# Hybrid encoder on one core: the double weight sum of a seven-product pair ahead of the split, a later DRAM round trip of the hidden tile, and VectorE's order around them

## What is computed

```
x = x + swiglu(rms_norm(x, ffn_norm[layer]), w_gate[layer], w_up[layer], w_down[layer])
def swiglu(xn, w_gate, w_up, w_down):
    return (silu(xn @ w_gate) * (xn @ w_up)) @ w_down
```

## Time and profile before

| | us |
|---|---|
| median of three runs | 2063.98 |
| the three runs | 2063.98, 2062.18, 2067.47 |
| the profiled execution's own time | 2068.36 |
| its span in the profile | 2066.6 |
| busy: TensorE | 2052.7 (99%) |
| busy: VectorE | 1725.8 (84%) |
| busy: ScalarE | 1131.4 (55%) |
| DMA: 452.72 MB, mean | 219 GB/s |

### The profile page before, as it was taken

How to read it: one execution, slowest core, us unless ns; L and a number is a source line. 1 busy time by engine, 2 the same in 40 slices (tenths; PEclk the granted TensorE clock), 3 DMA queues, 4 the chain that set the end, 5 groups by cost and what they waited for, 6 DMA issues and landing times.

```text
span 2066.6 us, 26692 instructions
## 1 busy us (share of the span) xinstructions
PE 2052.7 (99%) x9087; PEld 1693.5 (82%) x9087; DVE 1725.8 (84%) x2293; ACT 1131.4 (55%) x1483; POOL 77.1 (4%) x85
## 2 busy tenths in 40 slices
PE   9999999999999999999999999999999999999999
PEld 7888888888788888887888888888888877888887
DVE  5777669799999998878876776597999989988887
ACT  6465555555556554555555566555555555545453
POOL 0100011000000000000011000010000000000000
PEclk9999999999999999999999999999999999999999
DMA  8688666766777767766677775667676776776664
GB/s 278 214 279 255 207 212 197 221 212 217 222 238 220 227 223 227 224 206 213 206 223 245 237 220 153 202 198 219 214 223 218 219 235 215 224 234 204 222 199 159
DMA packets 252307, 452.72 MB, mean 219 GB/s; under 512 B 17840, under 2 KB 51760, under 8 KB 252208
## 3 DMA queue, kind: packets, MB, share of 16 engines
q1 hardware_dynamic: 249760, 447.24, 69.0%
q10 hardware_dynamic: 2448, 4.21, 0.6%
HBM read 422.81 MB, written 28.57 MB: 218 GB/s over the span
## 4 chain that ended last, share of the span: by engine, by line
PE 78%; DVE 10%; DMA 6%; issue 4%; ACT 1%; DVEq 0%; ACTq 0%; POOL 0%; SPq 0%
PE psum L959 16%; PE psum L961 16%; PE psum L960 16%; PE psum L831 9%; PE psum L834 9%; PE psum L832 9%; DMA w_raw<-in_w_up 4%; DVE w_lo L1463 2%; DMA w_raw<-in_w_down 1%; PE psum L885 1%; DVE stages L1880 1%; PE psum L899 1%; DVE ht_lo L1893 1%; DVE w_lo L1899 1%; DVE stages L1883 1%
## 5 line engine op out<-in xcount | busy, mean ns | idle before, releaser
L1066 ACT ACTIVATE w_hi<-w_raw 128x1024 fp32r<-128x1024 f32 x665 | 693.4, 1056 | 594.9 <-PE psum L834 212.9
L1463 DVE TENSOR_TENSOR w_lo<-w_raw,w_hi 128x1024 fp32r<-128x1024 f32 x587 | 702.4, 1219 | 213.7 <-ACT w_hi L1066 212.2
L959 PE MATMUL psum<-w_hi,xt_hi 128*128 128x512 f32 x1060 | 412.7, 389 | 0.8 <-DVE stages L1556 0.6
L960 PE MATMUL psum<-w_lo,xt_hi 128*128 128x512 f32 x1060 | 412.4, 389 | 0.0
L961 PE MATMUL psum<-w_hi,xt_lo 128*128 128x512 f32 x1060 | 412.4, 389 | 0.0
L831 PE MATMUL psum<-w_hi,xt_hi 128*128 128x512 f32 x604 | 243.2, 403 | 0.7 <-DVE w_lo L1463 0.6
L834 PE MATMUL psum<-w_hi,xt_lo 128*128 128x512 f32 x604 | 235.7, 390 | 0.0
L832 PE MATMUL psum<-w_lo,xt_hi 128*128 128x512 f32 x604 | 235.3, 389 | 0.0
L959 PEld LDWEIGHTS psum<-w_hi,xt_hi 128*128 128x128 f32 x1060 | 199.0, 188 | 42.8 <-issue 1.3
L961 PEld LDWEIGHTS psum<-w_hi,xt_lo 128*128 128x128 f32 x1060 | 199.0, 188 | 41.5
L960 PEld LDWEIGHTS psum<-w_lo,xt_hi 128*128 128x128 f32 x1060 | 199.0, 188 | 41.3
(11 more groups left out here) (248 smaller groups left out, 2702.3 us busy)
## 6 DMA issues: line engine op xcount, KB each, us to landing
w_raw<-in_w_gate SPq DMA_DIRECT2D x176, 512.0 KB, 4.4
w_raw<-in_w_up SPq DMA_DIRECT2D x176, 512.0 KB, 3.8
w_raw<-in_w_down SPq DMA_DIRECT2D x176, 512.0 KB, 5.3
w_raw<-in_cd_w_in SPq DMA_DIRECT2D x80, 512.0 KB, 4.5
w_raw<-in_ab_w_in SPq DMA_DIRECT2D x71, 512.0 KB, 4.6
block_dram<-turn_sb SPq DMA_DIRECT2D x42, 512.0 KB, 5.0
w_raw<-in_ab_w_out SPq DMA_DIRECT2D x32, 512.0 KB, 4.5
w_raw<-in_cd_w_out SPq DMA_DIRECT2D x32, 512.0 KB, 3.9
```

What stands on the lines that cost most here:

```text
L959: nc.tensor.matmul(acc, a_hi, b_hi, start=start, stop=False)
L960: nc.tensor.matmul(acc, a_hi, b_lo, start=False, stop=False)
L1066: nc.scalar.activation(w_hi[:, slot, 0:n, :], w_raw[:, slot, 0:n, :], ACT.Copy).then_inc(hi_ready, 1)
L1463: nc.vector.tensor_tensor(w_lo[:, slot], w_raw[:, slot], w_hi[:, slot].bitcast(F32), ALU.subtract).then_inc(lo_ready, 1)
```

## The change

1. `weight_sums` is cut in two. `first_sums` (the double sum) now stands ahead of `split_seven` (behind what finishes the earlier tiles at the same place); `other_sums` (third and fourth sum) stands behind the split. In the down stage `row_lows` goes in between third and fourth sum.
2. The round trip: TWIN becomes (12, UPU + 4, UPU + 8, UPU + 10): write to DRAM ahead of unit 4, read back ahead of unit 8, split at unit 10.
3. The 32x32 transposes (`hidden_blocks`) are taken out of `hidden` and stand behind the split of the same unit; they now store chunk by chunk (`chunk_blocks`, two instructions of 128x512, one for each token half, in place of one of 128x1024). For the down stage's first two residual tiles too.
4. With chunks contiguous, `hidden_hi` and `hidden_lo` are one instruction each in place of four.
5. `up_total_sum`, the first sum of `up_combine`, stands ahead of the split of unit 15; the next two swap places.
6. `row_sums` is cut in four parts, which in the down stage stand ahead of and behind the two units' splits before the pair; `combine` is put in an order in which neighbours do not depend on each other.

The core of the diff:

```diff
-FIRST, TWIN = (3, 11, 14, 15), (12, UPU + 1, UPU + 4, UPU + 8)
+FIRST, TWIN = (3, 11, 14, 15), (12, UPU + 4, UPU + 8, UPU + 10)
...
             def hidden_hi(layer, i):
                 act.wait_ge(landed, up_move(layer, i) * 64 + 64)
-                for c in range(4):
-                    dst = ht_hi[:, bass.ds(i * 4 + c, 1), :].rearrange("p c t -> p (c t)")
-                    ins = nc.scalar.activation(dst.rearrange("p (t a i) -> p t a i", t=TOK, a=4), turned_chunk(c), ACT.Copy)
-                    if c % 2:
-                        ins.then_inc(t_hi, 1)
+                nc.scalar.activation(hidden_chunks(ht_hi, i), turned_chunks(), ACT.Copy).then_inc(t_hi, 2)
...
             def hidden_lo(layer, i):
                 dve.wait_ge(landed, up_move(layer, i) * 64 + 64)
+                dve.wait_ge(t_hi, i * 2 + (ph["up", layer]["th"] + 2))
+                nc.vector.tensor_tensor(hidden_chunks(ht_lo, i), turned_chunks(), hidden_chunks(ht_hi, i).bitcast(F32),
+                                        ALU.subtract).then_inc(tile_split, 2)
...
+            def chunk_blocks(move, src):
+
+                dst = turn_sb[:].rearrange("p b (c t i) -> p t c b i", c=4, t=TOK)
+                blocks_of = src.rearrange("p t (c b j) -> p t c b j", c=4, b=4)
+                for tok in range(TOK):
+                    ins = nc.vector.transpose(dst[:, tok], blocks_of[:, tok])
+                ins.then_inc(blocks_ready, 1)
...
-            def weight_sums(u, a, s, sums):
+            def first_sums(u, a, s, sums):
...
                 dve.wait_ge(w_loaded[a], loads(u, a))
                 dve.wait_ge(w_loaded[b], loads(u + 1, b))
                 dve.wait_ge(tl_ready, s * 2 + 2)
-                b12, b22 = w_raw[:, b, 0, :], w_raw[:, b, 1, :]
+                b12 = w_raw[:, b, 0, :]
                 b11_b22 = w_raw[:].rearrange("p r c n -> p (r c) n")[:, UC * a:UC * a + 4:3, :]
                 nc.vector.tensor_tensor(raw[:, 0:2, :], b12.unsqueeze(1).broadcast_to([P, 2, N]), b11_b22,
                                         ALU.subtract).then_inc(t13_summed, 1)
...
+            def other_sums(u, a, s, sums, between=None):
+
+                raw, b22 = sums[0], w_raw[:, a + 1, 1, :]
                 dve.wait_ge(t13_summed, s + 1)
                 nc.vector.tensor_tensor(raw[:, 2, :], b22, raw[:, 0, :], ALU.subtract).then_inc(t2_summed, 1)
+                if between:
+                    between()
                 dve.wait_ge(t2_summed, s + 1)
                 nc.vector.tensor_tensor(raw[:, 3, :], w_raw[:, a, 1, :], raw[:, 2, :], ALU.subtract).then_inc(lo_ready, 1)
...
+                    if twin and p in up_sevens(i) and j == 0:
+                        if isinstance(i, int) and i == UP_FIRST:
+                            dve.wait_ge(x_stored, RES["down", layer] + 1)
+                        first_sums(u, idx % RING, up_sum(layer, i, UP_SEVEN.index(p)), UP_T)
+                    if twin and idx == COMBINE_AT:
+                        up_total_sum(layer, i, odd)
...
+                    if before and idx == before[0]:
+                        hidden_blocks(layer, i - 1, before != FIRST)
                     if twin and j == 0 and p in up_sevens(i):
-                        weight_sums(u, idx % RING, up_sum(layer, i, UP_SEVEN.index(p)), UP_T)
+                        other_sums(u, idx % RING, up_sum(layer, i, UP_SEVEN.index(p)), UP_T)
...
+                        next_rows(2 * j)
                         if not seven:
                             split(u, i % RING)
                         elif j == 0:
+                            first_sums(u, i % RING, down_sum(layer, d, p), sums)
                             split_seven(u, i % RING)
+                        if d == 0 and i == TENTH[0]:
+                            hidden_blocks(layer, HT - 1, True)
...
+                        next_rows(2 * j + 1)
```

More of the change, by code:

```diff
@@ L1514, in residual_blocks @@
                     dve.wait_ge(tile_split, split_count(layer, "down", 2 * n - 1))
-                blocks(residual_move(layer, name, n), stage[0], 4)
+                    chunk_blocks(residual_move(layer, name, n), stage[0])
+                else:
+                    blocks(residual_move(layer, name, n), stage[0], 4)
             def residual_lo(layer, name, n):
@@ L1580, in hidden @@
                     dve.wait_ge(acc_free[1], i * 2 + (2 * pu["b"] + 2))
-                if not (isinstance(i, int) and i == 0):
+                if isinstance(i, int) and i == 0:
+                    dve.wait_ge(blocks_out, up_move(layer, i) * 16)
+                else:
                     dve.wait_ge(tile_split, i * 2 + (split_count(layer, "up", 0) - 1))
-                blocks(up_move(layer, i), stage[2], 4)
+                chunk_blocks(up_move(layer, i), stage[2])
             def hidden_lo(layer, i):
                 dve.wait_ge(landed, up_move(layer, i) * 64 + 64)
[L1587 to L1594, removed]
+                dve.wait_ge(t_hi, i * 2 + (ph["up", layer]["th"] + 2))
+                nc.vector.tensor_tensor(hidden_chunks(ht_lo, i), turned_chunks(), hidden_chunks(ht_hi, i).bitcast(F32),
+                                        ALU.subtract).then_inc(tile_split, 2)
             def finish_up(layer, i, odd, twin, idx, kind):
@@ L1611, in finish_last, with up_total_sum @@
                     hidden_lo(layer, HT - 2)
-            def up_combine(layer, i, odd):
+            def up_total_sum(layer, i, odd):
                 c = up_combination(layer, i)
@@ L1845, in input_lo, with row_sums @@
                 fill_to_xt(h + 1, h % 2, 2 * h, 0, 2 * h)
-            def row_sums(r, p, rows, a_of, s_of):
+            def row_sums(r, part, p, rows, a_of, s_of):
                 pair = slice(UC * p, UC * p + UC)
[L1850 to L1853, removed]
                 a11, a12, a21, a22 = (a_of[:, c, tok * P:tok * P + P] for tok in range(TOK) for c in range(UC))
[L1855 to L1858, removed]
+                if part == 0:
+                    if r:
+                        dve.wait_ge(s_ready, r)
+                    nc.vector.tensor_tensor(a_of, rows[0][:, pair, :].bitcast(F32), rows[1][:, pair, :].bitcast(F32),
+                                            ALU.add).then_inc(rows_step, 1)
+                if part == 1:
+                    dve.wait_ge(rows_step, 3 * r + 1)
+                    nc.vector.tensor_tensor(s_of[:, 0, :], a21, a22, ALU.add).then_inc(rows_step, 1)
+                    nc.vector.tensor_tensor(s_of[:, 2, :], a21, a11, ALU.subtract)
+                if part == 2:
+                    dve.wait_ge(rows_step, 3 * r + 2)
+                    nc.vector.tensor_tensor(s_of[:, 1, :], s_of[:, 0, :], a11, ALU.subtract).then_inc(rows_step, 1)
+                if part == 3:
+                    dve.wait_ge(rows_step, 3 * r + 3)
+                    nc.vector.tensor_tensor(s_of[:, 3, :], a12, s_of[:, 1, :], ALU.subtract).then_inc(s_summed, 1)
             def row_lows(r, raw, high, low):
@@ L1929, in up_tile @@
                             r = (idx - 8) // 2
-                            row_sums(up_rows(layer, r), UP_ROWS[r], (xt_hi, xt_lo), DOWN_A[0], DOWN_S_RAW[0])
+                            for part in range(4):
+                                row_sums(up_rows(layer, r), part, UP_ROWS[r], (xt_hi, xt_lo), DOWN_A[0], DOWN_S_RAW[0])
+                    if before and idx == before[0]:
+                        hidden_blocks(layer, i - 1, before != FIRST)
                     if twin and j == 0 and p in up_sevens(i):
-                        if isinstance(i, int) and i == UP_FIRST:
-                            dve.wait_ge(x_stored, RES["down", layer] + 1)
-                        weight_sums(u, idx % RING, up_sum(layer, i, UP_SEVEN.index(p)), UP_T)
+                        other_sums(u, idx % RING, up_sum(layer, i, UP_SEVEN.index(p)), UP_T)
                     if twin and idx == COMBINE_AT:
```

43 lines of the change are left out of this document (33 added, 10 removed).

## The result

The changed kernel takes 2079.30 us in the median of four runs (2078.13 to 2081.23), beside 2063.08 for the kernel before (four runs). The ratio is 1.0074, 95% interval 1.0062 to 1.0085. The forecast was 2061.2 us with a range of 2057.2 to 2066.5; the time falls in that of rival B, which had a chance of 0.12 and a price of 2071 to 2080 us. The profiled execution took 2081.23 us by its own time, 12.9 more than that of before.

What follows compares the result with a forecast made beforehand. TensorE bounds the kernel, so only stops can be saved: 0.5 + 1.5 + 2.3 = 4.3 us, times 0.6 for a usual run 2.6, plus 0.6 for late loads; 2058.0 + 3.2 = 2061.2 us, range 2057.2 to 2066.5.

Steps and rivals of the forecast that it cites:

- rival B: Up tiles, pair 3: double sum waits for unit 7's load, holding up the split; 2071 to 2080 us, chance 0.12.
- What bounds the kernel: TensorE, busy 2052.7 of 2066.6 us; only its FFN stops can be saved, about 6 us in a usual run.
- the 2058.0 worked out for none: Whole kernel: the profiled execution's 2068.36 us less its 10.4 us of FFN stops.
- Double sum ahead at pair 1: Up tiles: the double sum fills VectorE's 0.46 us idle; half split's margin ahead of TensorE grows from 0.34 to about 1.0.
- The 0.7 us taken as a gain: Pair 1 of up tiles: VectorE's half split ends 0.7 us earlier, from a range of 0.11 to 1.14.
- Pair 3: Up tiles: the split stands behind the waiting double sum; margin falls from 1.21 to about 0.9 us (0.2 to 1.3).
- The term of 1.05 us: Pair 3: from unit 7's landing to the half split's end takes 6.7 us in place of 5.65, 1.05 longer.
- The limit of 4.5 us for the load: Pair 3: no stop from the new order as long as unit 7's load takes under 4.5 us.
- The round trip: Hidden tile's write and read-back moved off pair 1's loads: those 2 to 4 us earlier; both changes cut its stops 6.4 to 0.5.
- within 5: Sign to look for in the profile after: the load of unit 3 lands within 5 us.
- Smaller pieces: VectorE's hidden_lo, transposes and up_combine swap: 0.4 to 0.5 us saved in a tile of 41.5 us.
- Down stage: Double sum ahead of the split: between 0.1 won and 1.0 lost where the load is late; stops 3.0 to 2.3 us.

## Why the prediction was wrong

**What bounds the kernel: right.** Only stops could be won or lost, and the fastest versions sit at 2061.1 to 2061.4 with 2.7 to 4.7 us of stops, above the 2058.0 worked out for none. The windows it started from were misnamed, without harm: the first "up window" holds 144 us of the down stage (its loads start at 776 us) and the "down window" about 100 us of the next layer's attention; TensorE's idle time in them is all outside these parts.

**Double sum ahead at pair 1: right in the first tiles, worthless later.** In the second and third tiles with sevens of layer 0 the half split ended 1.54 and 1.10 us ahead of TensorE, as forecast (about 1.0). From the fourth on it was 0.05 to 0.7, and 0.05 is TensorE waiting. The 0.7 us taken as a gain was eaten by the ring, which by then ran behind TensorE.

**Pair 3: the step that failed.** "Net 0.35 less margin at pair 3: 1.21 to about 0.9 (0.2 to 1.3). No stop from that as long as the load takes under 4.5 us". The term of 1.05 us was right: from the double sum's release at 638.06 to the end of the half split at 644.75 it is 6.7 us, as worked out. What was wrong is what it was charged to. I set it once against a margin counted from a TensorE-bound start, helped by a pair 1 that would be early. But the load of unit 7 is issued by the half split of pair 1, so 3.65 + 6.7 = 10.35 us is a turn of a ring, to be set against TensorE's 10.20 in the same turn; it was over it with the load of 3.65 that the sum itself used, and is 10.81 with the measured 4.1 (both from issue to the double sum's release). A turn that is too long uses up any margin in front of it: 1.54 and 1.10 at pair 1, then 0.20 at pair 3, then stops in every tile. The limit of 4.5 us for the load should have been 3.5 (10.20 - 6.7).

**Rival B: right mechanism, wrong condition.** I made it depend on a load of 4.5 us or more, and gave it 0.12 for that. It needed no slow load: 4.26 us in the median was enough. That the time falls between its 2071 and 2080 is partly luck. Its price was 19 us at pair 3 alone, for loads of 5.2 us; pair 3 has 10.3 us of the stops, and 9.3 stand at pairs 1 and 5.

**The round trip: half right.** It does take stops off pair 1 (5.4 us at pair 1 before, none in the changed kernel with the double sum behind), and 11 us where the split waits for both loads. But alone it gained nothing, as unit 12 came late instead; and the load of unit 3 still took 5.7 us in the changed kernel (issued 620.33, landed 626.02), not "within 5", with the write right behind it. In the median of 18 tiles it went from 6.80 to 5.60 us, 1.2 us earlier and not 2 to 4. The load of unit 7, with the read-back right behind it, went from 3.62 to 4.26 in the median; I had charged the read-back to unit 8 alone.

**Smaller pieces: sized right, their worth not taken apart.** Together they may be worth something. The kernel that has them, with the sum behind in the up tiles, has 0.9981 and 4.7 us of stops; the new trip alone has 0.9999 and 8.4. The down stage's order is in that difference too, and the intervals just touch. One `hidden_lo` takes 1221 ns and one `hidden_hi` 1045 ns, the two transposes 689 each. The third sum starts 628.46 - 627.32 = 1.14 us behind the split, where it was 1.25 behind the double sum that it needs. The Trainium skill's rule ("VectorE: DVE Perf Modes", "The DRAIN you can't avoid"), by which the dependent wait costs nothing extra, is not borne out here by 0.11 us a step. The same section adds that an operation that is not held starts earlier, which the prediction left out. No run shows the kernel's time to depend on it.

**Down stage: about right.** Forecast 2.3 us (1 to 5), measured 2.8.

## What to carry to other kernels

Where an engine's result releases the load that the engine will wait for a few instructions later, count the whole turn (load, then all work from its landing to the release of the next) and set it against the bound engine's work in the same turn; a margin measured once says nothing if the turn is longer. An instruction that waits for a later arrival should stand behind whatever can be done without it: here the same work in the other order, and even the wait alone, cost 0.9 to 1.0% of the kernel. Less work on an engine that is not the bound (20.8 us here) is no gain while its waits lie in such a ring.

## What was not expected of the hardware

The load of 512 KB takes 3.4 us at the least and 4.6 in the median in the changed kernel, and how long it takes goes with the DMAs around it, those issued behind it included. The load of unit 7, in the median of 18 tiles, takes 3.60 to 3.62 us in the three kernels with the round trip at its old places, and 4.02 to 4.26 in the others, with the new ones, where the read-back is issued half a microsecond behind it. The load of unit 3 takes 6.59 to 6.84 us in the first three, with the write ahead of it and the read-back behind it, and 5.1 to 5.9 in the others. The cause inside the queues was not tried.
